# Unread products in TensorE's waits while a mixture-of-experts layer is being routed

## What is computed

```python
def moe_ffn(xn, router_w, router_b, w_gate, w_up, w_down):
    scores = sigmoid(xt @ router_w)              # 256 x 16
    sel = scores + router_b
    # best of 4 groups of experts by the sum of its two best, then the 2 best experts in it
    grp_score = sum(top_k(sel by group, 2)[0]);  gmask = one_hot(argmax(grp_score))
    _, eidx = top_k(where(gmask, sel, -inf), 2)
    gates = normalised scores of the two
    a = silu(xt @ w_gate[e]) * (xt @ w_up[e]) * gates
    return sum over e of a @ w_down[e]
```

## Time and profile before

| | us |
|---|---|
| median of 3 runs | 1691.22 (1690.06 to 1691.43) |
| profiled execution, its own time | 1693.3 |
| its span, first to last instruction | 1691.6 |
| TensorE busy | 1663.4 |
| VectorE busy | 748.2 |
| ScalarE busy | 484.6 |
| mean granted clock of TensorE, as a share of full | 0.998 |

### The profile page before, as it was taken

How to read it: one execution, slowest core, us unless ns; L and a number is a source line. 1 busy time by engine, 2 the same in 40 slices (tenths; PEclk the granted TensorE clock), 3 DMA queues, 4 the chain that set the end, 5 groups by cost and what they waited for, 6 DMA issues and landing times.

```text
span 1691.6 us, 20394 instructions
## 1 busy us (share of the span) xinstructions
PE 1663.4 (98%) x8539; PEld 1060.4 (63%) x8539; DVE 748.2 (44%) x1236; ACT 484.6 (29%) x624; POOL 54.5 (3%) x32
## 2 busy tenths in 40 slices
PE   9999999999999999999999999999999999999998
PEld 7888888887434444444469999988744444444343
DVE  6885477744123222222266777684522222222223
ACT  6444456434000000000054566664330000000000
POOL 3000000100000000000030000020000000000000
PEclk9999999999999999999999999999999999999999
DMA  9765656577999999999994545554699999999997
GB/s 302 248 198 168 198 157 202 172 258 270 389 398 426 428 428 427 427 427 427 427 347 143 157 137 157 191 188 153 247 416 399 425 427 428 427 428 427 426 428 293
DMA packets 111446, 533.78 MB, mean 316 GB/s; under 512 B 12629, under 2 KB 31609, under 8 KB 80889
## 3 DMA queue, kind: packets, MB, share of 16 engines
q1 hardware_dynamic: 110976, 532.28, 80.1%
q10 hardware_dynamic: 344, 0.13, 0.0%
q0 software_dynamic: 32, 0.02, 0.0%
HBM read 530.29 MB, written 2.11 MB: 315 GB/s over the span
## 4 chain that ended last, share of the span: by engine, by line
PE 93%; DMA 4%; DVE 1%; ACT 1%; issue 1%; DVEq 0%; ACTq 0%
PE PS L738 32%; PE PS L1055 24%; PE PS L1087 13%; PE PS L1017 7%; DMA DOUBLE<-in_moe_w_down 3%; PE PS L838 3%; PE PS L1030 2%; PE PS L1031 1%; PE PS L859 1%; PE PS L844 1%; PE PS L937 1%; PE PS L1220 1%; PE PS L1194 1%; PE PS L1199 1%; ACT AREA L1490 1%
## 5 line engine op out<-in xcount | busy, mean ns | idle before, releaser
L1671 DVE TENSOR_TENSOR LO<-ring,HI 128x2048 fp32r<-128x2048 f32 (+1 forms) x124 | 266.9, 2154 | 168.2 <-ACT HI L1301 167.8
L1055 PE MATMUL PS<-DOUBLE,AREA 128*64 128x512 f32 x1120 | 314.3, 595 | 0.0
L1301 ACT ACTIVATE HI<-ring 128x2048 fp32r<-128x2048 f32 (+1 forms) x124 | 223.7, 1804 | 267.5 <-PE PS L738 240.1
L738 PE MATMUL PS<-HI,XT_BOTH 128*128 128x512 f32 (+1 forms) x1344 | 297.9, 373 | 0.8 <-issue 0.6
L738 PEld LDWEIGHTS PS<-HI,XT_BOTH 128*128 128x128 f32 x1344 | 243.8, 188 | 35.3 <-issue 2.3
L1996 DVE TENSOR_TENSOR X<-PS,X 128x512 f32<-128x512 f32 x128 | 82.2, 685 | 308.0 <-PE PS L1031 308.0
L1055 PE MATMUL PS<-OVD,AREA 128*64 128x512 f32 x448 | 200.1, 595 | 0.0
L1055 PEld LDWEIGHTS PS<-DOUBLE,AREA 128*64 128x64 f32 x1120 | 95.4, 137 | 147.8 <-issue 147.3
L1087 PE MATMUL PS<-DOUBLE,AREA 128*64 128x512 f32 x672 | 170.3, 595 | 3.8 <-DMA DOUBLE<-in_moe_w_down 2.5
L738 PE MATMUL PS<-LO,XT_BOTH 128*128 128x512 f32 (+1 forms) x672 | 152.5, 368 | 0.0
L1017 PEld LDWEIGHTS PS<-AREA,XN 128*128 128x128 f32 x1024 | 118.4, 194 | 26.0 <-issue 24.3
(11 more groups left out here) (299 smaller groups left out, 1737.3 us busy)
## 6 DMA issues: line engine op xcount, KB each, us to landing
DOUBLE<-in_moe_w_gate SPq DMA_DIRECT2D x34, 2048.0 KB, 20.7
DOUBLE<-in_moe_w_up SPq DMA_DIRECT2D x26, 2048.0 KB, 21.3
DOUBLE<-in_moe_w_down SPq DMA_DIRECT2D x26, 2048.0 KB, 20.8
ring<-in_a_w_in SPq DMA_DIRECT2D x48, 1024.0 KB, 5.2
DOUBLE<-in_moe_w_down SPq DMA_DIRECT2D x32, 1024.0 KB, 10.2
OVD<-in_moe_w_down SPq DMA_DIRECT2D x12, 2048.0 KB, 20.2
ring<-in_b_w_in SPq DMA_DIRECT2D x32, 768.0 KB, 4.4
OVD<-in_moe_w_up SPq DMA_DIRECT2D x11, 2048.0 KB, 27.0
```

The costliest lines, as they stand in the source:

```text
L738: mm = pe.matmul(PS[:, banks[t], 0:n], lhs(k0 + kk, t)[part], weights[:, kk, 0:n], start=first and kk == 0 and p == 0, stop=last and kk == ...
L1055: last = pe.matmul(PS[64 * e:64 * e + 64, up, :], m_["XG"][:, c, 64 * e:64 * e + 64], slot(units[e])[:, kk, :], start=(c == 0), stop=(c == ...
L1301: act.activation(HI[s % 2][:, :, 0:n], ring[PLACE[u]][:, :, 0:n], ACT.Copy).then_inc(sem("hi_ready"), 1)
L1671: tt(LO[PLACE[u]][:, :, 0:n], ring[PLACE[u]][:, :, 0:n], HI[s % 2][:, :, 0:n], ALU.subtract)\
```

## The change

`keep_on` moves up in the text, so that `router_side` can call it, and five products are added in each layer. They are float32 products of ones with the first columns of `X` of token tile 0, without a semaphore. Three write bank 3: 128 columns before the wait of the second token tile in `turn(3)`, 384 before the wait in `logits(3)`, 256 before the wait in `logit_sums()`. Two write bank 0: 256 columns more before the wait for `mask_ready`, and 384 after the products for `counts`, which is before the first gather's wait for `SEL`.

```diff
@@ -751,10 +751,18 @@
             def CKT(k, t):
                 return CKH[:, k, t * P:(t + 1) * P], CKL[:, k, t * P:(t + 1) * P]
 
+            def keep_on(bank, *columns):
+
+
+                for n in columns:
+                    pe.matmul(PS[:, bank, 0:n], ONES, X[:, 0, 0:n], start=True, stop=True)
+
             def router_side(l, free, before):
 
                 def turn(b):
                     for t in range(NT):
+                        if b == 3 and t:
+                            keep_on(3, 128)
                         pe.wait_ge(sem(free), before + 2 * b + t + 1)
                         for k in range(4):
                             c = 4 * b + k
@@ -763,6 +771,8 @@
 
                 def logits(b):
 
+                    if b == 3:
+                        keep_on(3, 384)
                     pe.wait_ge(sem("x_columns"), 8 * l + 2 * b + NT)
                     for g in range(4):
                         c = 4 * b + g
@@ -774,6 +784,7 @@
 
                 def logit_sums():
 
+                    keep_on(3, 256)
                     pe.wait_ge(sem("parts_copied"), l + 1)
                     for t in range(NT):
                         last = pe.matmul(PS[:, 7, N_EXP * t:N_EXP * (t + 1)], PART[:, t * P:(t + 1) * P],
@@ -973,15 +984,9 @@
             logits(3)
             logit_sums()
 
-            def keep_on(bank, *columns):
-
-
-                for n in columns:
-                    pe.matmul(PS[:, bank, 0:n], ONES, X[:, 0, 0:n], start=True, stop=True)
-
             def route(l):
 
-                keep_on(0, 512, 512, 512)
+                keep_on(0, 512, 512, 512, 256)
                 pe.wait_ge(sem("mask_ready"), l + 1)
                 pe.matmul(PS[:, 1, 0:N_EXP], TRI_R[:, :], MK[:, 0, :], start=True, stop=True)
                 pe.matmul(PS[:, 1, N_EXP:2 * N_EXP], ONE_R[:, :], MK[:, 0, :], start=True, stop=False)
@@ -990,6 +995,7 @@
                 pe.matmul(PS[:, 5, 0:N_EXP], ONE_R[:, :], MK[:, 0, :], start=True, stop=False)
                 pe.matmul(PS[:, 5, 0:N_EXP], ONE_R[:, :], MK[:, 1, :], start=False, stop=True)\
                     .then_inc(sem("counts"), 1)
+                keep_on(0, 384)
 
             def turn_final(g):
                 for t in range(NT):
```

## The result

The changed kernel takes 1696.07 us (median of 8 runs, 1694.85 to 1696.83), the kernel before, in the same comparison, 1691.33 us. The ratio is 1.0024, with a 95% interval of 1.0015 to 1.0032. The forecast was 1689.4 us in a range of 1687.5 to 1691.6: wrong in sign and outside the range. Times above 1694.6 us had been given a chance of 0.03.

What follows compares the result with a forecast made beforehand. Clock dips in both layers' routing were taken to delay TensorE, before expert stages bound by the weight stream. Gains of 1.62 us (layer 0) and 0.20 us (layer 1) gave 1691.2 - 1.8 = 1689.4 us, range 1687.5 to 1691.6.

Steps and rivals of the forecast that it cites:

- each fits its own wait: Routing, layer 0: added products take 2.58 us in 3.29 us of TensorE's waits, so cost nothing at full clock.
- the 2.81 us wait without a releaser at 759 us: TensorE idle at 756 to 759 us kept its full clock; read as disagreeing with long gaps causing dips.
- (c): Routing: clock dip stays and meets the added products, making them slower; 1692.3 us, at the far end 1695.2; chance 0.07.
- (d): More gained than forecast: executions behind the median lose 1.62 us on both layers' gathers; 1687.8 us; chance 0.08.
- What the routing gains: Full clock shortens layer 0's gather by 1.62 us; layer 1's mask-to-gather stretch loses 0.20 us; 1.82 us in all.
- Whether it reaches the end: Transfer pauses in layer 0's first experts and layer 1's 1.4 us gap let both routing gains pass to the end.
- Rival (a): Routing: added products do not remove the clock dips, nothing is won; 1691.2 us; most of a 0.17 shared with another rival.
- The base of the sum: Unprofiled median of 1691.22 us, assumed to lose about as much to dips as the profiled execution.

Runs made afterwards that it cites:

- the run with 40 increments: Kernel before, plus 40 increments of an unread semaphore on TensorE's queue in layer 0, moving later code 40 places; 1698.1 us (ratio 1.0037).
- 22 increments: Kernel before, plus 22 increments of an unread semaphore on TensorE's queue in layer 0, moving later code; 1695.93 us (ratio 1.0021).
- 142: Kernel before, plus 142 increments of an unread semaphore on TensorE's queue in layer 0, moving later code; 1695.03 us, one run.
- 12 increments on the changed kernel: Changed kernel, plus 12 increments of an unread semaphore on TensorE's queue in layer 0, moving later code; 1690.4 us (0.999 of the kernel before).
- 160 increments: Kernel before, plus 160 increments of an unread semaphore on TensorE's queue in layer 0, moving later code; 1692.95 us (ratio 1.0005).
- 24: Changed kernel, plus 24 increments of an unread semaphore on TensorE's queue in layer 0, moving later code; 1690.55 us (0.9992 of the kernel before).

## Why the prediction was wrong

**The failed step** is the price of the added work at nothing because "each fits its own wait". It priced the 40 instructions by how long they run, and as nothing else. As to that, it was right: the stretch from the last transposes to the mask kept its 6.44 us. But they also move all the code behind them, and that cost 6.25 us at one branch (8.86 less 2.61), and about 2.0 us more by the clock's fall behind it. The row that bore on it was among mine: the 2.81 us wait without a releaser at 759 us. I read it as evidence on the clock, and never asked what TensorE was waiting for, though no row named a releaser. With that question, the 0.86 us wait at L1031 in layer 1 would have shown how near the next edge was. The Trainium skill, "Runtime: NRT & Kernel Launch", section "Instruction fetch mechanics", has a taken branch wait for its code. It would not have given the size, but it would have named the wait, and I did not weigh it.

**The rivals.** None had this mechanism. (c) came near the time, 1695.2 us at its far end, but by another way that the trace excludes: no dip met the added products, and all fit their waits at full clock. In (d) the two gathers are 2 x 1.62 = 3.24 us, so its time should have read 1688.0 us and not 1687.8; nothing hangs on it.

**What the routing gains: right in place and about right in size.** The forecast was 1.62 us in layer 0 and 0.20 us in layer 1, 1.82 us. The profile has 1.62 in layer 0 (5.46 less 3.84) and 0.21 in layer 1. That this profile has its slow gather in layer 0 was chance: which layer is hit differs, with both hit in the run with 40 increments. The 11 slow gathers in nine profiles make 1.2 a profile, about 2.0 us. With the code at equal places the medians differ by 2.0 us (1690.4 against 1692.44) and by 2.4 us (1696.07 against 1698.51, from different comparisons and only five runs of the second), a little more than one profile showed.

**Whether it reaches the end: right up to the branch of layer 1.** The last L1087 group before the branch of layer 1 ends 2.38 us earlier. 0.9 us of this is a shorter wait for a first load at the start, which differs from run to run, and the rest is the routings' gain: 0.86 + 1.62 + 0.21 would be 2.69 us, and 0.3 of it was lost on the way: behind layer 0's branch a dip made the first products take 5.28 us up to L1036 (756.74 to 762.02) where those of the kernel before took 3.58, and the waits for weights in layer 0's experts fell from 1.4 us to 0.2. The pauses in the transfers shrank as expected, 426 to 434 us from a share of 0.67 to 0.86:

```profile
426.00:434.00 8.00, 8.00 (x40) 1.00 0.86 318
```

**Where the 3.3 us more in the span come from**, between the two profiles: TensorE leaves the branch of layer 1 3.87 us later. Some 2.0 us are lost behind it at half the clock (1579.4 to 1583.4 us). Against this the wait at L1031, 0.86 us, is gone, and so is the wait of 1.7 us for down weights at the layer's end (the 0.2 us that the changed kernel still waits for them lie in layer 0). 3.87 + 2.0 - 0.86 - 1.7 = 3.3, as measured. The stream of weights, which ended about 2 us sooner (its share falls to 0.55 in 1670 to 1672 us, in the kernel before to 0.61 in 1672 to 1674), so gave back part of the loss.

**Rival (a)'s evidence, half wrong.** I had the 2.81 us gap with full clock stand against waits as a cause. In the changed kernel a gap of 2.73 us at the same branch of layer 0 did end in a dip, with products that start 0.87 us apart:

```profile
756.74 0.61 PE L1061 MATMUL PS<-SPARE,AREA 128*64 128x512 f32 x1 [2.73 <-issue]
...
758.58 1.06 PE L1061 MATMUL PS<-SPARE,AREA 128*64 128x512 f32 x1
```

So nearly the same gap brings a dip in one profile and none in another, and my rows showed one case only. The Trainium skill's rule that the prediction cites, "TensorE: Matmul & The Clock Gate", section "Why this matters for your kernels", is for longer gaps than either. So the prediction was wrong to say that the gap of 2.81 us disagrees with it; only the dips behind waits of at most 0.84 us do.

**The base of the sum** was a smaller error: 1691.22 us was the median of three runs. Over all comparisons the kernel before has medians of 1691.3 to 1692.2 us and single runs from 1689.5 to 1695.5. With that the range was too narrow by itself.

## What to carry to other kernels

An added instruction costs its run time and its place. In a kernel with a branch over a long block, look at where the target lies against the edges of the code's pieces, before and after any edit ahead of it; a wait without a releaser behind a branch is the sign. Unread products in waits do keep the clock up, and here they pay 1.5 to 2 us of 1691 by the medians, but a comparison of two kernels is a fair one only with the code behind them at the same place, and a few idle instructions are enough to see to that.

## What the runs showed of the hardware

- Behind a branch over some 740 instructions TensorE waits 2.4 to 3.1 us when the target has many places to the next edge, and 8.1 to 8.9 us when it has 2 to 5. With 17 to 42 places left the wait comes in two parts, the second of which ends 7.6 to 8.3 us after TensorE fell idle (7.6 in the kernel before, whose first wait begins at 1572.95 us and whose second ends at 1580.51; 8.3 with 22 increments; 7.95 with 142).
- The next piece does not follow at once. In the changed kernel's long wait (1570.6 to 1579.4 us) one packet of code starts within 1568.5 to 1571 us and the next only within 1575.5 to 1578, though the profile names nothing else that TensorE waited for. Rows of the instruction queue for these two stretches and for the whole wait; the columns are queue, packets, MB, share of 16 engines:

```profile
q8 instruction: 1, 0.02, 2.7%
...
q8 instruction: 1, 0.02, 2.5%
...
q8 instruction: 1, 0.02, 0.7%
```

What makes up the rest of the 8.9 us, and whether it would be shorter with the transfers idle, was not tried; in all of these runs the weights' stream was at 421 to 430 GB/s around the branches.
- The next piece comes as late where the wait is short. In the kernel before one packet of code starts within 1572 to 1573 us and the next within 1578 to 1579; with 12 increments on the changed kernel it is 1568 to 1569 and 1574 to 1575. The products of the first piece then run in between. Rows of the instruction queue for the first two of these stretches:

```profile
q8 instruction: 1, 0.02, 6.9%
...
q8 instruction: 1, 0.02, 6.9%
```

- Whether the clock falls behind a wait of 2.4 to 3.1 us differs from profile to profile: none behind 3.05 us in layer 0 with 160 increments, one behind 2.73 us in the changed kernel. The two kernels with all added products and short waits also scatter less: between 1689.1 and 1691.6 us in 10 runs with 12 increments, between 1689.7 and 1691.8 in 11 with 24, against 1689.5 to 1695.5 for the kernel before, which has many more runs.
